# Hybrid decoder layer on one core: x1 kept in DRAM while its tile holds weights, a later place for 5 MB of expert loads and for the constants

## The reference, cut to what matters

```python
h = rms_norm(x, g_mix); proj = h @ w_in                      # 1024 -> 2560: conv value, gate, q, k, v
conv_out = conformer_conv(c_val, c_gate, ...)                # GLU, 31 taps, LayerNorm, swish
attn = moba_attention(q, k, v)                               # 8 heads of 64
x = x + concat(rms_norm(conv_out), rms_norm(attn)) @ w_out   # called x1 below
h = rms_norm(x, g_ffn)
for e in range(32):                                          # top 1 of 4 groups, then top 2 of 8 experts
    hid = silu(h @ w_gate[e]) * (h @ w_up[e])                # 1024 -> 256
    y = y + gates[..., e:e + 1] * (hid @ w_down[e])          # 256 -> 1024
x = x + y                                                    # called x2
x = x + (p @ w_ple_proj) * sigmoid(rms_norm(x, g_ple) @ w_ple_gate + b_ple_gate)
return rms_norm(x, g_final)
```

## Time and profile before

| | before |
|---|---|
| time, median of 3 runs (lowest to highest) | 597.26 us (595.72 to 597.45) |
| time of the profiled execution | 595.68 us |
| its span | 593.8 us |
| PE busy | 506.3 us (85%) |
| DVE busy | 295.0 us (50%) |
| ACT busy | 185.4 us (31%) |
| moved by DMA | 146.10 MB, mean 246 GB/s |
| mean granted clock of TensorE | 0.945 of full speed |

### The profile page before, as it was taken

One profiled execution on the slowest core, in us unless ns is written; L12 is line 12 of the kernel. 1 busy time (PEld: TensorE's weight loads), 2 busy tenths in 40 slices (PEclk: granted clock), 3 DMA queues, 4 the chain that ended last, 5 costly groups with the idle time before them and its releaser, 6 DMA issues.

```text
span 593.8 us, 8744 instructions
## 1 busy us (share of the span) xinstructions
PE 506.3 (85%) x3193; PEld 299.7 (50%) x3193; DVE 295.0 (50%) x559; ACT 185.4 (31%) x355; POOL 77.9 (13%) x91
## 2 busy tenths in 40 slices
PE   1899999998879989945999989787777988899994
PEld 1688888775556668842433323222222332237883
DVE  2509989999996955484122121101111111167676
ACT  4832320325785352512011010000000000056655
POOL 0570000000032040010211111111110111000000
PEclk9999999999799989975999998888899888999998
DMA  8920400444505050594699999999999899748003
GB/s 336 387 77 2 146 11 8 155 155 161 216 1 214 1 214 35 187 415 167 257 416 421 417 419 422 418 411 419 400 396 420 357 395 413 313 185 331 1 1 141
DMA packets 34741, 146.10 MB, mean 246 GB/s; under 512 B 5776, under 2 KB 6032, under 8 KB 22928
## 3 DMA queue, kind: packets, MB, share of 16 engines
q1 hardware_dynamic: 28800, 133.72, 56.6%
q0 software_dynamic: 5328, 10.50, 4.7%
q10 hardware_dynamic: 576, 1.37, 0.6%
HBM read 140.85 MB, written 12.58 MB: 258 GB/s over the span
## 4 chain that ended last, share of the span: by engine, by line
PE 50%; SPq 20%; DMA 12%; DVE 8%; ACT 5%; issue 4%; POOL 1%; DVEq 0%; POOLq 0%; ACTq 0%
PE bank L1466 15%; SPq L563 9%; DMA wring<-w_up_in 8%; PE bank L1706 8%; PE bank L1770 7%; PE bank L1566 5%; SPq L570 4%; SPq L496 4%; PE bank L1490 4%; DMA wring<-w_in_in 2%; PE bank L1726 2%; PE bank L1749 2%; DMA arena<-rows_d,tfirst 1%; PE bank L1607 1%; DVE wring L1072 1%
## 5 line engine op out<-in xcount | busy, mean ns | idle before, releaser
L1706 PE MATMUL bank<-wring,arena 128*32 128x512 f32 x704 | 90.0, 670 | 20.3 <-DMA wring<-w_up_in 18.0
L1010 DVE SCALAR_TENSOR_TENSOR mix<-arena,pr,mix 128x512 f32<-128x512 f32 x120 | 86.6, 790 | 0.0
L1362 DVE TENSOR_TENSOR arena<-arena,bank 128x256 f32<-128x256 f32 x16 | 6.7, 421 | 141.7 <-ACT arena L898 141.7
L1706 PEld LDWEIGHTS bank<-wring,arena 128*32 128x32 f32 x704 | 27.5, 121 | 81.7 <-issue 76.9
L898 ACT ACTIVATE arena<-bank 128x256 f32<-128x256 f32 x16 | 6.2, 384 | 145.1 <-PE bank L1706 145.1
L1706 PE MATMUL bank<-mix,arena 128*32 128x512 f32 x240 | 40.4, 663 | 7.9 <-DMA arena<-w_up_in 7.9
L1726 PE MATMUL bank<-wring,arena 128*32 128x512 f32 x352 | 40.0, 595 | 5.3 <-ACT arena L901 5.3
L1706 PE MATMUL bank<-arena 128*32 128x512 f32 x80 | 40.3, 663 | 0.0
L1367 DVE COPY arena<-bank 128x512 f32<-128x512 f32 x16 | 11.1, 692 | 53.4 <-PE bank L1726 53.4
L1466 PE MATMUL bank<-hT_hi,win_hi 128*128 128x512 f32 x128 | 33.5, 398 | 1.9 <-DVE hT_lo L988 1.3
L1466 PE MATMUL bank<-hT_lo,win_hi 128*128 128x512 f32 x128 | 31.6, 389 | 0.0
(11 more groups left out here) (258 smaller groups left out, 901.4 us busy)
## 6 DMA issues: line engine op xcount, KB each, us to landing
wring<-w_gate_in SPq DMA_DIRECT2D x22, 1024.0 KB, 15.5
wring<-w_up_in SPq DMA_DIRECT2D x22, 1024.0 KB, 18.8
wring<-w_down_in SPq DMA_DIRECT2D x22, 1024.0 KB, 20.8
wring<-w_in_in SPq DMA_DIRECT2D x5, 2048.0 KB, 19.3
arena<-w_down_in SPq DMA_DIRECT2D x5, 1024.0 KB, 11.6
mix<-w_gate_in SPq DMA_DIRECT2D x5, 1024.0 KB, 15.1
mix<-w_up_in SPq DMA_DIRECT2D x5, 1024.0 KB, 17.2
arena<-w_gate_in SPq DMA_DIRECT2D x5, 1024.0 KB, 19.2
```

The lines of the kernel that those rows point to most:

```text
L1010: ins = dve.scalar_tensor_tensor(out=mixc[:, mm, :], in0=u[:, mm, j:j + S], scalar=w, in1=mixc[:, mm, :], op0=ALU.mult, op1=ALU.add)
L1706: ins = pe.matmul(pb[2 + s][lo:hi, :], xgT[:, s, k, lo:hi], up_w(w, a)[:, :, k, :], start=(k == 0), stop=(k == DK - 1))
```

## The change

1. **Constants.** ACT's queue now loads only the identity (128 columns of `c`) and `pr`. The other columns of `c` and `wr` are issued by SP behind the four pieces of `w_in`. The bias of the square roots is a tile `eps` of its own that DVE sets, and ACT does one unused square root first. What reads the rest of `c` waits for it: PE before `rotate(0)`, DVE before `turn(0)`; DVE waits for `wr` before it scales it.
2. **x1 to DRAM.** SP stores each row tile of x1 from `xs` to a new DRAM tensor `x1_d` as soon as it is complete, three before the loads of pass 1, the last before those of pass 2.
3. **Loads behind the first gathers.** Of the loads ahead, the second half of pass 2's up weights and `load_down(2, 2, 1)` are issued only when both first gathers have landed.
4. **The aside.** `xs` is then free, and takes the w_gate and w_up of the large expert of pass 3 (2 MiB), loaded right after, without a wait for pass 0. The reload of pass 3 leaves them out; PE reads them from `xs`.
5. **x1 back.** Behind `w_pg`'s first half SP loads `x1_d` into `xs`, and DVE waits for it before it adds y.

The core of the diff:

```diff
@@ block sync
             for i in (0, 1, 2, 4):
                 sp.dma_start(win[i], w_in_k[:, :, i * 512:(i + 1) * 512]).then_inc(win_loaded[i], 16)
+            sp.dma_start(c[:, P:C_MASK], cst[:, P:C_MASK]).then_inc(const_loaded, 16)
+            sp.dma_start(c[:, C_MASK:C_END], cst[:, C_MASK:C_END]).then_inc(const_loaded, 16)
+            sp.dma_start(wr[:], w_r.rearrange("(p k) n -> p k n", k=DK)).then_inc(wr_loaded, 16)
...
+            x1_rows = x1_d.rearrange("(t p) n -> p t n", p=P)
             sp.dma_start(bias_row, bias_d.rearrange("n a -> (a n)").partition_broadcast(P)).then_inc(rbias_loaded, 16)
+            for t in range(TT - 1):
+                for half in range(2):
+                    banks.wait_emptied(sp, ("outc", 2 * t + half))
+                sp.dma_start(x1_rows[:, t], xs[:, t, :]).then_inc(x1_stored, 16)
             banks.wait_full(sp, ("outc", 2 * TT - 1))
             load_up(1, 1, 1)
             for a in range(2):
                 load_down(1, 1, a)
-            for a in range(2):
-                load_up(2, 2, a)
+            for half in range(2):
+                banks.wait_emptied(sp, ("outc", 2 * TT - 2 + half))
+            sp.dma_start(x1_rows[:, TT - 1], xs[:, TT - 1, :]).then_inc(x1_stored, 16)
+            load_up(2, 2, 0)
+            for s in range(2):
+                sp.wait_ge(gathered[s], 16)
+            load_up(2, 2, 1)
...
                 for a in range(2):
-                    load_up(w, n, a)
+                    if not aside(n, a):
+                        load_up(w, n, a)
...
             banks.wait_emptied(sp, "owner")
+            sp.wait_ge(x1_stored, 16 * TT)
+            sp.wait_ge(xn_ready, 2 * TT - 1)
+            sp.wait_ge(last_rows, 1)
+            for kh in range(2):
+                banks.wait_emptied(sp, ("h2", TT - 1, kh))
+            for i, src in enumerate((w_gate, w_up)):
+                sp.dma_start(up_aside()[:, i],
+                             src[bass.ds(expert(SLOTS, 0), 1)].rearrange("e (p k) n -> p (e k) n", k=DK)
+                             ).then_inc(aside_loaded, 16)
             rounds = STRAIGHT // SLOTS
-            with sp.Fori(1, rounds) as i:
+            for w in range(SLOTS):
+                reload(SLOTS + w, w, w)
+            with sp.Fori(2, rounds) as i:
...
             sp.dma_start(wpg[0], pg[:, :, 0:512]).then_inc(pg_loaded[0], 16)
+            sp.dma_start(xs[:], x1_rows).then_inc(x1_loaded, 16)
@@ block scalar
-            act.dma_start(c[:, 0:C_MASK], cst[:, 0:C_MASK]).then_inc(const_loaded, 16)
-            act.dma_start(c[:, C_MASK:C_END], cst[:, C_MASK:C_END]).then_inc(const_loaded, 16)
+            act.dma_start(c[:, 0:P], cst[:, 0:P]).then_inc(ident_loaded, 16)
             act.dma_start(pr[:], prm).then_inc(prm_loaded, 16)
-            act.dma_start(wr[:], w_r.rearrange("(p k) n -> p k n", k=DK)).then_inc(prm_loaded, 16)
-            eps = c[:, C_EPS:C_EPS + 1]
+            act.wait_ge(eps_set, 1)
+            act.activation(unused[:], eps[:], ACT.Sqrt)
...
-            act.wait_ge(const_loaded, 32)
@@ block vector
+            dve.memset(eps[:], EPS).then_inc(eps_set, 1)
...
+            dve.wait_ge(const_loaded, 32)
             turn(0)
-            dve.wait_ge(const_loaded, 32)
+            dve.wait_ge(wr_loaded, 16)
...
             split_gate(0)
+            dve.wait_ge(x1_loaded, 16)
@@ block tensor
-            pe.wait_ge(const_loaded, 32)
+            pe.wait_ge(ident_loaded, 16)
...
-                pe.wait_ge(up_loaded[w], 64 * loads)
+                pe.wait_ge(up_loaded[w], 64 * loads - (32 if w == 0 and not (isinstance(n, int) and n < SLOTS) else 0))
+                if aside(n, 0):
+                    pe.wait_ge(aside_loaded, 32)
...
+                        weights = up_aside() if aside(n, a) else up_w(w, a)
```

More of the change, by code:

```diff
@@ L91 @@
 C_NUM = C_COL + 2
-C_EPS = C_NUM + 4 * TT
-C_END = C_EPS + 1
+C_END = C_NUM + 4 * TT
 PM = TAPS + 4
@@ L250, in build @@
         lnr = sb("lnr", [P, S])
+        eps = sb("eps", [P, 1])
+        unused = sb("unused", [P, 1])
         mean_w = sb("mean_w", [P, P])
@@ L367, in slot_of, with aside, up_aside @@
             return n % SLOTS if n < STRAIGHT else (STRAIGHT % SLOTS, (STRAIGHT + 1) % SLOTS)[n % 2]
+        def aside(n, a):
+            return isinstance(n, int) and n == SLOTS and a == 0
+        def up_aside():
+            return xs[:].rearrange("p t n -> p (t n)").rearrange("p (w k n) -> p w k n", w=2, k=DK)
         def up_w(w, a):
@@ L742, in mean_root @@
                 act.wait_ge(root_ready, 2 * (which * TT + t) + 1)
-                act.activation(ss[:, which, t:t + 1], sq[:, which, t:t + 1], ACT.Sqrt, scale=1.0 / D, bias=eps).then_inc(root_ready, 1)
-            act.wait_ge(const_loaded, 32)
+                act.activation(ss[:, which, t:t + 1], sq[:, which, t:t + 1], ACT.Sqrt, scale=1.0 / D, bias=eps[:]).then_inc(root_ready, 1)
             for t in range(TT):
@@ L841, in _ @@
             banks.wait_full(act, "attn_sq")
-            emptied(act.activation(gss[:, 1, :], bk("attn_sq")[:, 0:TT], ACT.Sqrt, scale=1.0 / CH, bias=eps), "attn_sq")
+            emptied(act.activation(gss[:, 1, :], bk("attn_sq")[:, 0:TT], ACT.Sqrt, scale=1.0 / CH, bias=eps[:]), "attn_sq")
             for m in range(CM):
@@ L850, in _ @@
             banks.wait_full(act, "var")
-            emptied(act.activation(lnr[:], bk("var")[:], ACT.Sqrt, bias=eps), "var")
+            emptied(act.activation(lnr[:], bk("var")[:], ACT.Sqrt, bias=eps[:]), "var")
             for m in range(CM):
@@ L861, in _ @@
             banks.wait_full(act, "conv_sq")
-            emptied(act.activation(gss[:, 0, :], bk("conv_sq")[:, 0:TT], ACT.Sqrt, scale=1.0 / CH, bias=eps), "conv_sq")
+            emptied(act.activation(gss[:, 0, :], bk("conv_sq")[:, 0:TT], ACT.Sqrt, scale=1.0 / CH, bias=eps[:]), "conv_sq")
             for t in range(TT):
```

17 lines of the change are left out of this document (12 added, 5 removed).

## The result

The changed kernel takes 588.33 us in the median of 4 runs (587.78 to 590.82), the kernel before 597.36 us in 4 runs. The ratio is 0.9856, with a 95% interval of 0.9831 to 0.9880: 8.6 us faster, between 7.2 and 10.1. The prediction said 586.8 us, in a range of 583.4 to 592: direction and range were right, the gain was 1.5 us too large. The profiled execution took 588.65 us, its span 586.8, against a span of 593.8 before. That is 7.0 us and not 9; where the 2 us between lie is read under e1.

The account below looks back on a forecast made before the run. The prediction took the expert passes to be bound by one stream of DMA bytes and the start by a landing; 3.1 + 4.5 + 2.9 = 10.5 us off the median of 597.26 gave 586.8 us, range 583.4 to 592.

Parts of the forecast that it names:

- Edit 1, 3.1 us: Start: with 1.22 MB less ahead of w_in's first piece, it lands at 14.3 instead of 17.34, 3.1 us earlier.
- The 3.1 us go through to PE: Start: the landing stays last, behind transposes ending by 13.7, so PE and all of the kernel move 3.1 us earlier.
- rival (d): Tail: x1's load holds up the rows of `y_d`, PE idles and its clock falls; slower, 601.3 us, chance 0.03.
- Edit 3, 4.5 us: First gather: with fewer bytes ahead it takes 3.7 us instead of 8.2, winning 4.5 us, ends 0 and 5.5.
- nearly done: First gather: the load queue ends at 266 to 267, so the gather issued at 262.86 meets it almost finished.
- the quiet one, plus about one us: First gather: its time is the last scatter's 2.7 us on quiet DMA plus about one us of remaining traffic, 3.7.
- Rival (a): First gather: it keeps its 8.2 us, taking turns with loads still moving; 591.3 us, chance 0.11.
- Edit 4, 2.9 us: Reloads: the aside moves 2.10 MB from the stream into the gap ahead of it, winning 2.9 us, ends 2 and 5.2.
- Edit 5, nothing: Tail: reading x1 back adds 5.2 us of bytes but costs nothing; the other end is 2.1 us lost.
- rival (b): Tail: it takes 2.1 us back, if the last scatter shares a busy DMA; 588.9 us, chance 0.06.
- 3.6 us of slack: Tail: DVE's first sum is done at 533.05 and PE needs it at 536.67, so 3.6 us are to spare.
- (c): Passes: the stream waits for PE's up matmuls at a later reload, only its earlier start counts; 589.7 us, chance 0.05.

Follow-up runs that it names:

- e1: The kernel before with the constants edit alone: 594.89 us, ratio 0.9942 to the kernel before.
- e3: The kernel before with only the last 3 MiB of loads ahead of the passes put behind the first gathers: 593.89 us, ratio 0.9905 to the kernel before.
- e6: The changed kernel without the load of x1 from DRAM and DVE's wait for it: 589.03 us, ratio 0.9818 to the kernel before.
- e4: The changed kernel with x1 read back in two halves, the second behind the first rows of y: 588.23 us, ratio 0.9828 to the kernel before.
- e9: e4 with the first two pieces of w_in loaded in halves by columns, first halves first: 586.67 us, ratio 0.9805 to the kernel before.
- e2: The changed kernel without the two waits for the gathers: 591.54 us, ratio 0.9882 to the kernel before.
- e5: The changed kernel with all four loads of pass 2's up weights behind the gathers, so 7 MiB wait: 590.76 us, ratio 0.9868 to the kernel before.
- e8: e4 with more unused transposes on PE between the logits and pass 0: 586.26 us, ratio 0.9810 to the kernel before.
- e10: e4 with the edits of e8 and e9 together: 585.51 us, ratio 0.9772 to the kernel before.

## Why the prediction was right or wrong

**Edit 1, 3.1 us.** Right on the landing: 14.1 to 14.6 in the nine profiles with this edit and w_in in whole pieces, against 17.3 in before and e3: 2.7 to 3.2 us, 3.0 in the mean. That the landing stays last held too, and so did its limit: the transposes ended at 13.2, below the predicted 13.7. "The 3.1 us go through to PE" held only in part. The same edit made PE idle for 3.0 to 4.0 us ahead of its first product, its granted clock fell to 0.50 to 0.72 over the next six us, and 0.8 of the 3.0 us were lost again (0.1 to 1.4, ACT's first `mix<-bank` under e1). The prediction put that at nothing, though its rival (d) names the same effect for the tail.

**Edit 3, 4.5 us.** The mechanism was right, the size was not. The queue was not "nearly done" at the gather's issue. In the changed kernel's profile DMA was full when the gather was issued at 262.03, and for 3 us after:

```profile
255.00:262.00 7.00, 2.31 (x29) 2.03 (x29) 5.60 (x23) 0.20 (x1) 0.00 (x0) 0.58 1.02 425
262.00:265.00 3.00, 2.17 (x11) 2.02 (x12) 2.69 (x13) 0.00 (x0) 2.08 (x2) 0.50 1.01 429
266.00:267.00 1.00, 0.00 (x0) 0.00 (x0) 0.86 (x5) 0.00 (x0) 0.00 (x0) 0.50 0.45 168
```

The prediction's own sum says the same: it has the bulk end at 266 to 267, 3 to 4 us after the gather's issue at 262.86, and then allows "about one us of remaining traffic". The gather took 5.5 and 4.9 us in its two profiles, 5.1 in the mean of the six kernels with 6 MiB ahead whose PE was left alone (the changed one twice, e3, e6, e4, e9), not 3.7. Against the mean of 8.5 in before, e1 and e2 that is 3.4 us, not 4.5. The term that failed is "the quiet one, plus about one us". On an empty queue the gather takes at most 3.4 us (e5, where PE came to it only then), so the bytes still moving added at least 1.5 to 2.1. Whether a quiet gather is as fast as the scatter's 2.7 us, which the prediction took for it, no run shows.

**The turns between queues.** Rival (a) let the gather keep its 8.2 us; it fell. The rule behind it is the Trainium skill's, from "DMA: Bandwidth & Descriptors", section on queues, rings and completion order, that each DMA engine takes turns between the queues that have work: it agrees with the runs. 8.2 to 8.8 us with 9 MiB ahead, 4.9 to 5.5 with 6 MiB that end during the gather (5.7 and 5.8 in e8 and e10), at most 3.4 with 4 MiB that were done before it: what counts is how long other packets still move while it does.

**Edit 4, 2.9 us.** From pass 0 to pass 15 it is 229.1 to 231.2 us with the aside (changed twice, e2, e4, e6, e9), 232.9 to 233.8 without (before, e1, e3): 3.3 us in the means, 230.1 against 233.4. Slightly more than predicted and less than the 5.2 us of its bytes, and for the reason given: DMA's share before the second reload is 0.89. One detail was off: PE, not the landing, bound the seventh pass, and the stream took over at the eighth.

**Edit 5, nothing.** Wrong by 0.9 us, seen in all four profiles with x1 loaded in one piece (71.4 to 72.1 us of tail, against 70.9 to 71.0 in the others). x1's bytes landed when they should: 6.0 us after `ple` began, 5.8 by the prediction. What it missed is that the last scatter took 5.4 us beside them, so the rows were issued 6.5 us after `ple` in place of 3.8. The prediction gave the scatter's 5.4 us a place (rival (b)), but checked the wrong consumer. I gave DVE's first sum 3.6 us of slack, and it was in time: PE turned the first tile right behind `ple`. But PE turns the second tile next. Before, its sum was done 13.6 us after `ple` began (533.86 + 2.60, from DVE's timeline, against 522.86), and PE came to it about 1 us after the turns began at 13.8: 1.2 us of slack. Now the sum is done at 16.1 (528.51 + 2.60 - 515.04), 2.5 us later, and PE waits 1.28 us for it. With 0.4 us saved behind that, 0.9 are left.

**The sum.** 3.0 - 0.8 + 3.4 + 3.3 - 0.9 = 8.0 us, against 10.5 predicted; measured were 9.0 in the medians and 8.6 by the ratio (7.2 to 10.1). The steps that failed are edit 3's size (1.1 us), edit 5 (0.9) and the clock behind edit 1 (0.8); edit 4 gave 0.4 more than predicted. That the total lay in the range is owed in part to its width, 8.6 us. None of rivals (a), (c) and (d) came about; (b) did, at 0.9 of its 2.1 us.

**Its own signs.** Of the three signs of being wrong, the gather's (over 8 us) did not show. The first reload did: it came 4.0 us earlier in the first profile and 5.0 in the second (281.15), not 7 to 8, by the terms given with the rows above. The third showed in part: PE waited 1.28 us for the second sum. One reading was loose as well: in slice 31 of the passes DMA is at 8 tenths (357 GB/s), not 9.

## What to carry to other kernels

Where a stage is one stream of bytes, look for the idle stretch ahead of it and put bytes there; but count only up to where the queue runs dry again, and a byte moved out of an earlier busy stretch costs its full time in the stream later. A short transfer on the critical path is worth protecting from bulk loads, up to the point where its protection leaves DMA idle (here 5 MiB behind the gathers won, 7 MiB lost, part of it because both gathers were waited for). Work that comes to PE earlier in one piece and late in the next leaves PE idle between them: look at the granted clock behind such a gap before you count the whole gain. When a load is added near the end of a queue, check every consumer behind it in its engine's order, not just the first.
